# The SBUF buffers of a two-block transformer kernel in a new order

## The chip, the cores and the metric

The kernel runs on one core of a Trainium2 chip. The metric is the device time of one execution in microseconds.

## The reference

Input x has 256 tokens of 1,024 features. The first block has two layers. Each is an FFN, a mixer of four attention kinds, and another FFN:

```
x = x + 0.5 * swiglu(rms_norm(x, g1), w_gate, w_up, w_down)      # D_FF = 2816
pa, pb, pc, pd = split(rms_norm(x, gm) @ w_in)                   # 2464 columns
x = x + concat([neighbourhood(pa), mla(pb), diff(pc), gqa(pd)]) @ w_out
x = x + 0.5 * swiglu(rms_norm(x, g2), w_gate2, w_up2, w_down2)
x = rms_norm(x, gf)
```

The second block is one layer on the same tokens:

```
u = rms_norm(x, g) @ w_in_2                                      # 7424 columns
ya, yb, yc = pool(u) * silu(.), sliding_window(u) * silu(.), block_attention(u) * silu(.)
merged = ga * (ya @ w_proj_a) + gb * (yb @ w_proj_b) + gc * (yc @ w_proj_c)
out = rms_norm(x + merged @ w_out_2, gf_2)
```

All of it is float32.

## The kernel before

x stays in SBUF transposed (xT, 8 chunks of 128 features by 256 tokens). Nearly all of the work is products of activations with weights that are read once. A product of float32 numbers is made of three products of the faster type float32r: each factor is split into a high part (its rounded value) and a low part (the rest), and `product` adds high x high, high x low and low x high in PSUM. In the profile these are lines 442, 445 and 446, and 486, 489 and 494 where a stage begins with the high parts alone.

Weights come in slots of 128 partitions x 2,048 columns (1 MB), three slots deep. For slot r, SyncE loads raw[r % 3] (line 360) once the slot three before it has been split, ScalarE writes the high part w_hi[r % 3] (line 888) once the slot has landed and TensorE has begun an earlier slot, and VectorE writes the low part w_lo[r % 3] (line 1213). There are 81 slots for each of the two layers, and 45 for the last block. A full slot of 256-wide products is 48 matmuls.

Who streams and who is stationary depends on the stage. In the FFNs (gate, up, down), in the output product of the mixers and in the last block's z, gate and branch products, the weights are stationary (128 columns at a time) and hT (normed activations, transposed) or act (the gated product) streams, 256 columns. In the token projections ("proj", "tproj", function `token_proj`) hT is stationary and the weights stream, 256 columns. In the last block's output product the weights stream, 512 columns at a time. In the profile a group is named out<-streamed,stationary.

The order of the steps of a mixer is written out by hand (ORDER, ORDER2), and every engine runs through it in its own queue, with semaphores between them. The FFNs are loops.

Buffers in SBUF are made by `sb(...)` in the order of the program text, each at the next multiple of 32 bytes behind the one before. The first one, xT, begins at byte 4,224 of each partition: 4,096 bytes for descriptors (`dynamic_dma_scratch_size=4096` in the call) and four small constants lie ahead of it. PSUM tensors and all views of the buffers are unchanged by the diff.

Of the kernel before, what the change touches and what calls it, by code (L numbers as in the profile page):

```python
# [7 lines left out]
F32R = mybir.dt.float32r  # L8
# [5 lines left out]
P = 128  # L14
S = 256
T = S // P
# [17 lines left out]
PW = W1  # L34
# [4 lines left out]
RING = 3  # L39
SLOT = 2048  # L40
# [8 lines left out]
I_ID, I_MC, I_MS, I_GC, I_GS, I_NA, I_MB, I_MM, NCONST = 0, 128, 192, 256, 384, 512, 576, 832, 1088  # L49
# [84 lines left out]
def build(nc, a):  # L134
    with ExitStack() as ctx:
        def sb(name, shape, dt=F32):
            return ctx.enter_context(nc.sbuf_tensor(name, shape, dt))
# [2 lines left out]
            return ctx.enter_context(nc.semaphore(name))  # L140


        xT = sb("xT", [P, DC, S])
        hn = sb("hn", [P, T, D])
        hT_hi = sb("hT_hi", [P, DC, S], F32R)
        hT_lo = sb("hT_lo", [P, DC, S], F32R)
        act_hi = sb("act_hi", [P, 2, 2, S], F32R)
        act_lo = sb("act_lo", [P, 2, 2, S], F32R)
        proj = sb("proj", [P, T, PW])
        up_buf = sb("up_buf", [P, 2048])  # L150
        qkT = [sb(f"qkT{i}", [P, 8, S]) for i in range(2)]
        probs = [sb(f"probs{i}", [P, 4, S]) for i in range(2)]
# [1 line left out]
        bias_buf = sb("bias_buf", [P, 3072])  # L154
        scratch = sb("scratch", [P, 1536])
        pooledT = sb("pooledT", [P, 4, S])
        row = sb("row", [P, NROW])
        cols_buf = sb("cols", [P, L + 1, NCOL])
        gain2 = sb("gain2", [P, L, DC])
        const = sb("const", [P, NCONST])  # L160
        stat = sb("stat", [P, 96])
        half = sb("half", [P, 32])
        ones = sb("ones", [P, P])
        smx = sb("smx", [P, 2, 4])
        ssum = sb("ssum", [P, 2, 4])
        sinkx = sb("sinkx", [P, 2, 4])
        lam = sb("lam", [P, 4])
        xr = sb("xr", [P, 4])
        diag = sb("diag", [P, 4, P])
        mla_rope = sb("mla_rope", [P, 2, T * 2 * 32])  # L170
        r_row = sb("r_row", [P, 2, S])
        raw = [sb(f"raw{i}", [P, SLOT]) for i in range(RING)]
        w_hi = [sb(f"w_hi{i}", [P, SLOT], F32R) for i in range(RING)]
        w_lo = [sb(f"w_lo{i}", [P, SLOT], F32R) for i in range(RING)]

        t5 = qkT[0][0:32, 0:3, :].rearrange("p c s -> p (c s)")

# [1686 lines left out]
```

How the kernel before makes its waits and increments, by code:

```python
        def wait_tr_full(eng, f):  # L306
            eng.wait_ge(tr_full[f % 2], f // 2 + 1)
# [1 line left out]
        def wait_tr_done(eng, first, n):  # L309
            for f in range(max(first, first + n - 2), first + n):
                eng.wait_ge(tr_free[f % 2], f // 2 + 1)
# [1 line left out]
        def wait_pj_full(eng, f):  # L314
            eng.wait_ge(pj_full[f % 2], f // 2 + 1)
# [1 line left out]
        def wait_pj_free(eng, f):  # L317
            eng.wait_ge(pj_free[f % 2], f // 2 + 1)
# [24 lines left out]
        @block.sync  # L343
# [14 lines left out]
            def load(slot_view, src, r, l, i=None):  # L358
                sp.wait_ge(lo_set, number_of(r, l, i))
                sp.dma_start(slot_view, src).then_inc(raw_in[r % RING], 16)
# [11 lines left out]
                with sp.Fori(0, FB // 2) as i:  # L372
                    for k in range(2):
                        pos = base + 2 + 3 * k
                        load(colslot(pos), cols(wg, l, i * 512 + (k + 1) * 256), pos, l, i)
                        load(colslot(pos + 1), cols(wu, l, i * 512 + (k + 1) * 256), pos + 1, l, i)
                        load(rowslot(pos + 2), rows(wd, l, i * 512 + k * 256), pos + 2, l, i)
                load(rowslot(base + 32), rows(wd, l, (FB - 1) * 256), base + 32, l)
            for l in range(L):
                ffn(l, FFN1_AT, a["ffn1_w_gate"], a["ffn1_w_up"], a["ffn1_w_down"])
                sp.wait_ge(rpb_skew[l], 16 * 8)
                sp.dma_start(bias_buf[:, 1536:3072], a["rpb_skewed"][l]).then_inc(nab_in, 16)
                if l == 0:
                    sp.wait_ge(t5_skew, 16)
```

## Time and profile before

| | us |
|---|---|
| median of 3 runs | 1352.24 |
| lowest, highest | 1350.92, 1352.86 |
| profiled execution, its time | 1345.35 |
| its span, first to last instruction | 1343.1 |
| TensorE busy | 1293.2 |
| VectorE busy | 834.5 |
| ScalarE busy | 640.0 |
| GpSimd busy | 76.4 |

The mean granted TensorE clock of the profiled execution is 0.977. Matmuls overlap, so TensorE's busy time says only that one was under way; how fast they follow each other is read from their starts or from their count in a window.

### The profile page before, as it was taken

Reading aid. Unit: us, or ns where it says so; the run is one execution under the profiler, and the core shown is the slowest. Engines: PE = TensorE matmul, PEld = TensorE weight load, DVE = VectorE, ACT = ScalarE, POOL = GpSimd, SP = SyncE. Lnnn points to the kernel's source line nnn. Section 1 sums busy time; section 2 is a strip of 40 time slices with the busy share of each in tenths; the row PEclk is TensorE's granted clock in tenths of the full one; section 3 lists DMA queues with packets and bytes.
Section 4 is the critical chain, followed back from the end, with each engine's and each line's share of the span. In section 5 each row is a group of like instructions: output and inputs, shape, how many; then the busy total and the mean of one; then the engine's idle time right before and its main releaser. Section 6 shows DMA issues by size and latency. Waiting matters only on the chain.

```text
span 1343.1 us, 24747 instructions
## 1 busy us (share of the span) xinstructions
PE 1293.2 (96%) x10496; PEld 1266.5 (94%) x10496; DVE 834.5 (62%) x1057; ACT 640.0 (48%) x850; POOL 76.4 (6%) x57
## 2 busy tenths in 40 slices
PE   6999999988999999999999997999999989999997
PEld 6999999987999999999999996899999989899996
DVE  5755567755665555875557675586555664446665
ACT  4433346745533334533334764553333544666542
POOL 1110011200000000000001120000000000000000
PEclk9999999987999999999999997899999999999999
DMA  8776565320565555565565540256555655415542
GB/s 281 222 208 201 184 220 156 126 94 4 186 189 188 187 187 181 165 198 188 187 201 156 166 139 29 67 181 193 188 187 187 196 158 178 136 50 161 182 146 108
DMA packets 169514, 220.34 MB, mean 164 GB/s; under 512 B 5280, under 2 KB 152480, under 8 KB 169312
## 3 DMA queue, kind: packets, MB, share of 16 engines
q1 hardware_dynamic: 165680, 213.66, 50.0%
q0 software_dynamic: 2080, 2.48, 0.9%
q10 hardware_dynamic: 1680, 3.13, 0.7%
q8 instruction: 56, 0.92, 0.3%
q14 instruction: 18, 0.15, 0.0%
HBM read 218.15 MB, written 3.42 MB: 165 GB/s over the span
## 4 chain that ended last, share of the span: by engine, by line
PE 86%; ACT 6%; DVE 5%; issue 1%; DMA 1%; POOL 0%; SPq 0%; POOLq 0%; DVEq 0%; ACTq 0%
PE pj L442 12%; PE pj L446 12%; PE pj L445 12%; PE acc L442 8%; PE acc L446 8%; PE acc L445 8%; PE tr L442 6%; PE tr L446 6%; PE tr L445 6%; PE acc L625 3%; ACT probs L1016 2%; DVE w_lo L1213 1%; ACT w_hi L888 1%; PE tr L617 1%; PE acc L605 1%
## 5 line engine op out<-in xcount | busy, mean ns | idle before, releaser
L1213 DVE TENSOR_TENSOR w_lo<-raw,w_hi 128x2048 fp32r<-128x2048 f32 (+2 forms) x206 | 458.4, 2226 | 249.2 <-ACT w_hi L888 247.8
L888 ACT ACTIVATE w_hi<-raw 128x2048 fp32r<-128x2048 f32 (+2 forms) x206 | 380.8, 1852 | 419.4 <-PE pj L442 151.0
L442 PE MATMUL pj<-hT_hi,w_hi 128*128 128x256 f32 x992 | 279.7, 282 | 1.3 <-DVE w_lo L1213 1.1
L446 PE MATMUL pj<-hT_hi,w_lo 128*128 128x256 f32 x992 | 278.2, 280 | 0.0
L445 PE MATMUL pj<-hT_lo,w_hi 128*128 128x256 f32 x992 | 278.1, 280 | 0.0
L446 PE MATMUL acc<-act_hi,w_lo 128*128 128x256 f32 x704 | 197.3, 280 | 0.0
L442 PE MATMUL acc<-act_hi,w_hi 128*128 128x256 f32 x704 | 197.3, 280 | 0.0
L445 PE MATMUL acc<-act_lo,w_hi 128*128 128x256 f32 x704 | 197.3, 280 | 0.0
L442 PEld LDWEIGHTS pj<-hT_hi,w_hi 128*128 128x128 f32 x992 | 186.9, 188 | 2.8 <-DVE w_lo L1213 1.3
L445 PEld LDWEIGHTS pj<-hT_lo,w_hi 128*128 128x128 f32 x992 | 186.9, 188 | 0.0
L446 PEld LDWEIGHTS pj<-hT_hi,w_lo 128*128 128x128 f32 x992 | 186.8, 188 | 0.0
L442 PE MATMUL tr<-hT_hi,w_hi 128*128 128x256 f32 x640 | 181.1, 283 | 2.4 <-DVE scratch L1317 2.4
L445 PE MATMUL tr<-hT_lo,w_hi 128*128 128x256 f32 x640 | 180.1, 281 | 0.0
L446 PE MATMUL tr<-hT_hi,w_lo 128*128 128x256 f32 x640 | 180.1, 281 | 0.0
L442 PEld LDWEIGHTS acc<-act_hi,w_hi 128*128 128x128 f32 x704 | 132.6, 188 | 0.0
L445 PEld LDWEIGHTS acc<-act_lo,w_hi 128*128 128x128 f32 x704 | 132.6, 188 | 0.0
L446 PEld LDWEIGHTS acc<-act_hi,w_lo 128*128 128x128 f32 x704 | 132.6, 188 | 0.0
L442 PE MATMUL pj<-w_hi,hT_hi 128*128 128x256 f32 (+1 forms) x448 | 127.9, 285 | 0.5 <-ACT proj L1039 0.5
L446 PE MATMUL pj<-w_hi,hT_lo 128*128 128x256 f32 (+1 forms) x448 | 126.3, 282 | 0.0
L445 PE MATMUL pj<-w_lo,hT_hi 128*128 128x256 f32 (+1 forms) x448 | 125.9, 281 | 0.0
L442 PEld LDWEIGHTS tr<-hT_hi,w_hi 128*128 128x128 f32 x640 | 121.3, 190 | 3.7 <-DVE scratch L1317 3.3
L445 PEld LDWEIGHTS tr<-hT_lo,w_hi 128*128 128x128 f32 x640 | 121.2, 189 | 0.3 <-issue 0.2
(214 smaller groups left out, 1970.6 us busy)
## 6 DMA issues: line engine op xcount, KB each, us to landing
raw<-in_w_in SPq DMA_DIRECT2D x47, 1024.0 KB, 5.4
raw<-in_ffn_w_up SPq DMA_DIRECT2D x44, 1024.0 KB, 5.4
raw<-in_ffn_w_down SPq DMA_DIRECT2D x44, 1024.0 KB, 5.0
raw<-in_ffn_w_gate SPq DMA_DIRECT2D x43, 1024.0 KB, 5.4
raw<-in_w_out SPq DMA_DIRECT2D x12, 1024.0 KB, 4.9
raw<-in_w_proj_a SPq DMA_DIRECT2D x4, 512.0 KB, 3.5
raw<-in_w_proj_b SPq DMA_DIRECT2D x4, 512.0 KB, 3.5
raw<-in_w_proj_c SPq DMA_DIRECT2D x4, 512.0 KB, 3.4
```

The source lines that it names most:

```text
L442: ins = pe.matmul(out, lhs[0], rhs[0], start=first, stop=False, **kw)
L445: pe.matmul(out, lhs[0], rhs[1], start=False, stop=False, **kw)
L446: return pe.matmul(out, lhs[1], rhs[0], start=False, stop=last, **kw)
L605: ins = pe.matmul(ps[:, h, 0:nk * P], q, k, start=True, stop=True)
L617: ins = pe.transpose(bank[:, j, :], probs[u % 2][:, h, kt * P:(kt + 1) * P], ident)
L625: ins = pe.matmul(ps[:, 0, h * 64:(h + 1) * 64], probsT[u % 2][:, h, kt, :], v(h, kt), start=(kt == 0), stop=(kt == nk - 1))
L888: act.activation(w_hi[r % RING][:, 0:w], raw[r % RING][:, 0:w], ACT.Copy).then_inc(hi_set, 1)
L1016: ins = act.activation(probs[u % 2][:, h, 0:nk * P], src[:, h, 0:nk * P], ACT.Exp, bias=smx[:, u % 2, h:h + 1], scale=scale, accum_out=ssu ...
L1213: dve.tensor_tensor(w_lo[r % RING][:, 0:w], raw[r % RING][:, 0:w], w_hi[r % RING][:, 0:w].bitcast(F32), ALU.subtract).then_inc(lo_set, 1)
```

## The change

The buffers are made in another order: first the large ones whose size is a multiple of 2,048 bytes, with the nine weight buffers (raw, w_hi, w_lo) right behind act_lo, then proj, then the small ones. Sizes, views, instructions, waits and transfers stay the same. The last byte used is the same within 32.

```
-        proj = sb("proj", [P, T, PW])
+        raw = [sb(f"raw{i}", [P, SLOT]) for i in range(RING)]
+        w_hi = [sb(f"w_hi{i}", [P, SLOT], F32R) for i in range(RING)]
+        w_lo = [sb(f"w_lo{i}", [P, SLOT], F32R) for i in range(RING)]
         up_buf = sb("up_buf", [P, 2048])
         qkT = [sb(f"qkT{i}", [P, 8, S]) for i in range(2)]
         probs = [sb(f"probs{i}", [P, 4, S]) for i in range(2)]
...
         bias_buf = sb("bias_buf", [P, 3072])
         scratch = sb("scratch", [P, 1536])
         pooledT = sb("pooledT", [P, 4, S])
+        diag = sb("diag", [P, 4, P])
+        r_row = sb("r_row", [P, 2, S])
+        proj = sb("proj", [P, T, PW])
+        const = sb("const", [P, NCONST])
+        ones = sb("ones", [P, P])
+        stat = sb("stat", [P, 96])
+        half = sb("half", [P, 32])
+        mla_rope = sb("mla_rope", [P, 2, T * 2 * 32])
         row = sb("row", [P, NROW])
         cols_buf = sb("cols", [P, L + 1, NCOL])
         gain2 = sb("gain2", [P, L, DC])
-        const = sb("const", [P, NCONST])
-        stat = sb("stat", [P, 96])
-        half = sb("half", [P, 32])
-        ones = sb("ones", [P, P])
         smx = sb("smx", [P, 2, 4])
         ssum = sb("ssum", [P, 2, 4])
         sinkx = sb("sinkx", [P, 2, 4])
         lam = sb("lam", [P, 4])
         xr = sb("xr", [P, 4])
-        diag = sb("diag", [P, 4, P])
-        mla_rope = sb("mla_rope", [P, 2, T * 2 * 32])
-        r_row = sb("r_row", [P, 2, S])
-        raw = [sb(f"raw{i}", [P, SLOT]) for i in range(RING)]
-        w_hi = [sb(f"w_hi{i}", [P, SLOT], F32R) for i in range(RING)]
-        w_lo = [sb(f"w_lo{i}", [P, SLOT], F32R) for i in range(RING)]
```

The starts in bytes, worked out from the sizes (float32 and float32r have 4 bytes) and the rule of 32 above:

| buffer | size | before | mod 2048 | mod 64 | after | mod 2048 | mod 64 |
|---|---|---|---|---|---|---|---|
| xT | 8192 | 4224 | 128 | 0 | 4224 | 128 | 0 |
| hn | 8192 | 12416 | 128 | 0 | 12416 | 128 | 0 |
| hT_hi | 8192 | 20608 | 128 | 0 | 20608 | 128 | 0 |
| hT_lo | 8192 | 28800 | 128 | 0 | 28800 | 128 | 0 |
| act_hi | 4096 | 36992 | 128 | 0 | 36992 | 128 | 0 |
| act_lo | 4096 | 41088 | 128 | 0 | 41088 | 128 | 0 |
| raw0 to raw2 | 3 x 8192 | 142304 | 992 | 32 | 45184 | 128 | 0 |
| w_hi0 to w_hi2 | 3 x 8192 | 166880 | 992 | 32 | 69760 | 128 | 0 |
| w_lo0 to w_lo2 | 3 x 8192 | 191456 | 992 | 32 | 94336 | 128 | 0 |
| up_buf to pooledT | 63488 | 64896 | 1408 | 0 | 118912 | 128 | 0 |
| diag | 2048 | 137184 | 2016 | 32 | 182400 | 128 | 0 |
| r_row | 2048 | 140256 | 992 | 32 | 184448 | 128 | 0 |
| proj | 19712 | 45184 | 128 | 0 | 186496 | 128 | 0 |
| const | 4352 | 131648 | 576 | 0 | 206208 | 1408 | 0 |
| ones | 512 | 136512 | 1344 | 0 | 210560 | 1664 | 0 |
| stat | 384 | 136000 | 832 | 0 | 211072 | 128 | 0 |
| half | 128 | 136384 | 1216 | 0 | 211456 | 512 | 0 |
| mla_rope | 1024 | 139232 | 2016 | 32 | 211584 | 640 | 0 |
| row | 2568 | 128384 | 1408 | 0 | 212608 | 1664 | 0 |
| cols | 588 | 130976 | 1952 | 32 | 215200 | 160 | 32 |
| gain2 | 64 | 131584 | 512 | 0 | 215808 | 768 | 0 |
| smx, ssum, sinkx, lam, xr | 128 | 137024 | 1856 | 0 | 215872 | 832 | 0 |

In the last line the start is that of smx; ssum and lam begin 32 bytes past a multiple of 64 in both orders. The group from up_buf to pooledT keeps its inner order.

## Rows read from the trace of the kernel before

**Rows 1.** Part 1 of the page: busy us, share of the span, instructions.
```profile
PE 1293.2 (96%) x10496; PEld 1266.5 (94%) x10496; DVE 834.5 (62%) x1057; ACT 640.0 (48%) x850; POOL 76.4 (6%) x57
```

**Rows 2.** The chain that ended last, shares of the span by engine.
```profile
PE 86%; ACT 6%; DVE 5%; issue 1%; DMA 1%; POOL 0%; SPq 0%; POOLq 0%; DVEq 0%; ACTq 0%
```

**Rows 3.** Line 442: durations (ns min/median/max), first and last start, forms; who waited.
```profile
L442 PE MATMUL pj<-hT_hi,w_hi x992: 277/281/468, 17.6 to 1303.0; 128*128 128x256 f32 x199
...
L442 PE MATMUL pj<-w_hi,hT_hi x448: 235/281/682, 209.8 to 1190.5; 128*128 128x256 f32 x140, 128*128 128x160 f32 x10
...
  ACT w_hi L888: 405.5, 125
```

**Rows 4.** Windows: length, busy us and count by engine, granted clock, DMA share, GB/s.
```profile
366.00:548.00 182.00, 182.00 (x1536) 181.99 (x1534) 113.97 (x102) 77.08 (x62) 0.00 (x0) 1.00 0.57 184
892.00:1074.00 182.00, 182.00 (x1535) 182.00 (x1534) 113.75 (x102) 76.94 (x62) 0.00 (x0) 1.00 0.59 190
557.00:728.00 171.00, 171.00 (x1458) 170.92 (x1457) 111.99 (x114) 69.09 (x49) 3.51 (x1) 1.00 0.60 191
...
1126.50:1310.00 183.50, 179.66 (x1511) 175.82 (x1510) 103.64 (x172) 105.09 (x168) 0.00 (x0) 1.00 0.45 140
```

**Rows 5.** Timeline, TensorE: start us, duration us, instruction; ends of two runs.
```profile
1114.95 0.28 PE L442 MATMUL pj<-w_hi,hT_hi 128*128 128x256 f32 x1
...
1126.47 0.28 PE L442 MATMUL pj<-hT_hi,w_hi 128*128 128x256 f32 x1
...
1323.07 0.40 PE L442 MATMUL acc<-w_hi,hT_hi 128*128 128x512 f32 x1
...
1334.04 0.40 PE L446 MATMUL acc<-w_hi,hT_lo 128*128 128x512 f32 x1
```

**Rows 6.** TensorE's groups by form: count, busy us, mean ns, idle before, releaser.
```profile
L442 PE MATMUL pj<-hT_hi,w_hi 128*128 128x256 f32 x992 | 279.7, 282 | 1.3 <-DVE w_lo L1213 1.1 <-DVE scratch L1608 0.2
L442 PE MATMUL acc<-act_hi,w_hi 128*128 128x256 f32 x704 | 197.3, 280 | 0.0
L442 PE MATMUL tr<-hT_hi,w_hi 128*128 128x256 f32 x640 | 181.1, 283 | 2.4 <-DVE scratch L1317 2.4
L442 PE MATMUL pj<-w_hi,hT_hi 128*128 128x256 f32 x416 | 119.1, 286 | 0.5 <-ACT proj L1039 0.5
...
L442 PE MATMUL acc<-w_hi,hT_hi 128*128 128x512 f32 x32 | 12.8, 399 | 0.0
```

**Rows 7.** VectorE's and ScalarE's groups by form, same columns.
```profile
L1303 DVE TENSOR_TENSOR act_lo<-proj,act_hi 128x512 fp32r<-128x512 f32 x44 | 30.5, 692 | 1.5
L1299 DVE TENSOR_TENSOR proj<-proj,r_row 128x512 f32<-128x512 f32 x44 | 30.5, 692 | 1.5
...
L888 ACT ACTIVATE w_hi<-raw 128x2048 fp32r<-128x2048 f32 x190 | 363.1, 1915 | 414.0 <-PE pj L442 145.5 <-PE acc L442 135.2 <-PE tr L442 119.3
...
L900 ACT ACTIVATE hn<-xT 128x2048 f32<-128x2048 f32 x7 | 13.3, 1903 | 0.0
```

**Rows 8.** DMA issues: count, KB each, median us from issue to landing.
```profile
raw<-in_ffn_w_up SPq DMA_DIRECT2D x44, 1024.0 KB, 5.4
raw<-in_ffn_w_down SPq DMA_DIRECT2D x44, 1024.0 KB, 5.0
...
t_skewed<-t_line POOLq DMA_DIRECT2D x1, 768.0 KB, 10.8
```

**Rows 9.** Waits of ScalarE: us in total, times, longest us.
```profile
ACT w_hi L888 <- DMA raw<-in_ffn_w_gate: 6.1, 2, 5.0
```

**Rows 10.** The chain that ended last, near the start: start us, us, what.
```profile
5.10 8.18 DMA raw<-in_ffn_w_up
```

**Rows 11.** The same chain in layer 0's mixer.
```profile
254.00 0.87 PE tr L617 x8
```

## The prediction

> **What bounds the kernel now.** The page's busy table comes first: TensorE is busy for 1293.2 of 1343.1 us, VectorE for 62% and ScalarE for 48% [rows 1]. The chain that ended last agrees: 86% of it is TensorE, 6% ScalarE, 5% VectorE, 1% DMA [rows 2]. So the time is mostly the number of matmuls times the distance from one start to the next. A matmul's recorded duration doesn't give that distance: it is 281 ns at the median whether hT or the weights stream through the array [rows 3], and the next matmul has long begun when it ends. The spacing has to be counted, in stretches where TensorE never stops.
>
> - First FFN of layer 1 (hT or act streams, weights are stationary), 557 to 728 us: 1,458 matmuls touch the window, about two of them begun before it, so 171.0 / 1,456 = 117.4 ns [rows 4].
> - Second FFN, 366 to 548 us in layer 0 and 892 to 1074 in layer 1, the same code on the same buffers: 182.0 / 1,534 = 118.6 ns [rows 4].
> - Token projections of the last block (weights stream, hT is stationary): tproj 4 and tproj 2 have 96 matmuls between the starts at 1114.95 and 1126.47 us, 120.0 ns [rows 5].
> - Last product, 512 columns wide, weights stream: 47 matmuls between 1323.07 and 1334.04 us, 233.4 ns [rows 5].
>
> The granted clock is 1.00 in these windows, the 2.4 GHz level, at which 256 columns are 106.7 ns and 512 are 213.3. So a 256-column product takes 10.7 to 13.3 ns more than its columns, and the 512-column one 20.1 ns more. That excess is what a change of addresses could touch. It is large: the three big groups with hT or act streaming hold (992 + 704 + 640) x 3 = 7,008 matmuls, and the one with weights streaming 416 x 3 = 1,248 [rows 6]. One nanosecond on these 8,256 is 8.3 us, 0.6%. I leave the smaller groups out of the sums.
>
> **The change, part by part.** No instruction, wait or transfer is added, removed or reordered, so all counts stay. Only the starts move. By the table of starts, raw, w_hi and w_lo go from 32 past a multiple of 64 bytes (992 modulo 2048) to a multiple of 64 (128 modulo 2048); diag, r_row and mla_rope also lose their 32; hT and act stay put; cols, ssum and lam stay 32 past. Four kinds of user follow.
>
> *VectorE and ScalarE.* The trace holds both placements already. A 512-column product with r_row, 32 bytes off, takes 692 ns, and the one with only aligned buffers (act_lo) 692. ScalarE's 2048-column pass over a slot, 32 off, takes 1915 ns, the aligned one over xT 1903 [rows 7]. So the price is 0 to 12 ns an instruction. Even 12 ns on all 190 copies of slots is 2.3 us of ScalarE time, under 414.0 us of idle time ahead of them [rows 7], most of it spent waiting for TensorE (405.5 us in 125 waits [rows 3]). I take 0; without that cover it would be a gain of up to 2.3 us.
>
> *Transfers.* A 1 MB slot lands 5.0 to 5.4 us after its issue [rows 8], one is needed every 48 x 117.4 ns = 5.6 us, and it is asked for ahead of need: the largest group of ScalarE's waits for a slot's landing is 6.1 us in two waits [rows 9]. Exposed is only the start, where the chain holds 8.18 us of the second slot's load [rows 10]. At the 5.0 us of the same size elsewhere it would save 3.2 us; at 10.8, the longest landing of any transfer [rows 8], it would lose 2.6. Those are the ends; I take 0, since that load is slow for company (eight loads of xT and of the first slot are issued just before it), not for its target. The Trainium skill ("DMA: Bandwidth & Descriptors", How a descriptor splits into AXI transactions) says a descriptor that starts off a multiple of 256 bytes costs extra beats: my estimate from that page is 39 beats for 1,024 bytes at the old offset and 36 at the new one. No row here shows beats; by it the exposed load would gain under a microsecond.
>
> *GpSimd and small tables.* GpSimd works on stat, half and xr, a few columns each, and is 1% or less of the chain [rows 2]; 0.
>
> *TensorE's reads.* Here the trace speaks on both sides. For an effect: weights streaming, 32 off, against an aligned hT go at 120.0 ns, while an aligned hT streaming against off-placed weights goes at 117.4 or 118.6, with the same shape, type and pattern of three products [rows 4, 5]. Only addresses and roles differ. Against an effect: first and second FFN read the very same addresses and still differ by 1.2 ns, so something besides placement (how loads and matmuls fall into step after a stop) picks the level too. And within 557 to 728 us halves and chunks of a slot set the two operands at distances that differ by multiples of 512 bytes, while VectorE is busy for 112 us and ScalarE for 69, and the level holds.
>
> The Trainium skill ("SBUF — State Buffer", Who interferes with whom) gives TensorE two independent read ports and says it never waits on anyone; by it no layout has a price and the sum is zero. The windows agree as far as other engines' work goes; they don't decide between TensorE's own two reads.
>
> I take the favourable step: once all operands of these products start on a multiple of 64, long runs go at 117.4 ns, the lowest spacing that a 256-column product holds over a stretch here.
> - Token projections: 1,248 x 2.6 ns = 3.2 us.
> - The two second FFNs: 2 x 1,534 x 1.2 ns = 3.7 us.
> - Last block: 15 z and gate slots of 48 and 12 branch slots of 24 follow the start at 1126.47 us, 1,008 matmuls among the 1,511 of that window [rows 4]; I assume 118.6 for them, x 1.2 = 1.2 us.
> - The 512-column product: 32 x 3 x an assumed 2 ns = 0.2 us.
>
> The sum is 8.3 us. The profiled execution took 1345.35 us with a span of 1343.1, and would take 1337. The median of the runs shown is 1352.24, 6.9 above it, so the forecast is 1352.2 - 8.3 = **1344 us**, with 1340 to 1349 as that case's own range (upper end: the token projections alone gain).
>
> **Rivals.**
>
> *Nothing happens.* How a run falls into step sets the level, and it falls as before. For it: the two FFN levels repeat in both layers at equal addresses, and VectorE and ScalarE don't care about 32 bytes. Against it: the token projections stand apart at 120.0. Time 1352. One stretch that falls otherwise by chance moves it by 1,534 x 1.2 = 1.8 us.
>
> *Slower: the two operands now start in the same place.* hT and a weight chunk will begin at equal offsets modulo 512; so far they differ by 352. If TensorE's two reads get in each other's way when they start together, the good level is lost. All at 120.0 costs (7,008 - 3,068 - 1,008) x 2.6 = 7.6 and 4,076 x 1.4 = 5.7, together 13.3 us: 1366. It decides against the change as soon as the two first FFNs fall by one step (2 x 1,456 x 1.2 = 3.5 us, 1356), more than the token projections could give back. For it: equal code can run at 118.6. Against it: shifts of 512 bytes between the operands do nothing today.
>
> *Much faster: the whole excess is the 32 bytes.* The nearest row of a low spacing is 8 transposes of 128 columns, all operands aligned, in 0.87 us, 109 ns each [rows 11]. All 8,256 products going from some 118.3 to 109 would give 77 us: 1275; half of it 1314. For it: an excess that grows with width (10.7 or more at 256, 20.1 at 512) needs a cause. Against it: where hT or act streams, the streamed operand is aligned already and the excess is there; and an excess per column is no sign of a start address. The Trainium skill ("TensorE: Matmul & The Clock Gate", Back-to-back issue gap) gives the columns plus 2.5 ns for an isolated matmul, 109.2 ns here; no FFN product of the trace keeps to it.
>
> **How the numbers follow.** What a measurement of this kernel can tell from no change is 0.2%, 2.7 us. The forecast has a chance of 0.36, much faster 0.08, nothing 0.34, slower 0.22. A little of the forecast's case ends within the bound (one gain alone), and a little of "nothing" outside it, so: faster 0.43, same 0.35, slower 0.22. The range reaches over no change into both outer cases, past the two first FFNs' loss on one side and the half-way value of "much faster" nearly on the other: 1322 to 1359. About 0.15 is left out.
>
> **What would show it.** After the change: the 96 matmuls of tproj 4 and 2 in 11.27 us in place of 11.52; about 1,550 matmuls in 182 us of the second FFN in place of 1,536; the last product's spacing below 233 ns. VectorE's and ScalarE's times for a slot and the 5.0 to 5.4 us to landing stay. The prediction is wrong if the three spacings stay where they are (nothing) or the first FFN leaves 117.4 upward (slower). Its mechanism is wrong, whatever the time, if a gain comes from the start or from ScalarE's waits for transfers.

## The result: slower by 0.7%

| kernel | median us | lowest, highest | executions |
|---|---|---|---|
| before | 1351.93 | 1344.61, 1358.19 | 12 |
| after | 1361.90 | 1355.08, 1367.87 | 12 |

The ratio is 1.0073, with a 95% interval of 1.004 to 1.0106. The profiled execution of the changed kernel took 1367.55 us with a span of 1365.2 and a mean granted clock of 0.968. The forecast was 1344 and the range 1322 to 1359: the rival "slower" came true.

All line numbers of the product are one higher than before (L443, L446, L447). The page's busy table and the shares of the chain that ended last:

```profile
PE 1317.2 (96%) x10496; PEld 1291.1 (95%) x10496; DVE 834.5 (61%) x1057; ACT 639.8 (47%) x850; POOL 76.4 (6%) x57
...
PE 86%; ACT 6%; DVE 5%; issue 1%; DMA 1%; POOL 0%; SPq 0%; POOLq 0%; DVEq 0%; ACTq 0%
```

The counts are those of [rows 1] and the shares those of [rows 2]. Only TensorE grew, by 24.0 us of busy time. The groups by form of VectorE and ScalarE, which answer to [rows 7]:

```profile
L1304 DVE TENSOR_TENSOR act_lo<-proj,act_hi 128x512 fp32r<-128x512 f32 x44 | 30.5, 693 | 1.5
L1300 DVE TENSOR_TENSOR proj<-proj,r_row 128x512 f32<-128x512 f32 x44 | 30.5, 692 | 1.5
...
L889 ACT ACTIVATE w_hi<-raw 128x2048 fp32r<-128x2048 f32 x190 | 362.7, 1912 | 428.8 <-PE pj L443 153.8 <-PE acc L443 143.9 <-PE tr L443 122.5
...
L901 ACT ACTIVATE hn<-xT 128x2048 f32<-128x2048 f32 x7 | 13.3, 1900 | 0.0
```

A pass over a slot that no longer sits 32 bytes off takes 1912 ns where it took 1915, and the product with r_row stays at 692: these two engines show no effect of the move. The transfers of a slot, beside [rows 8]:

```profile
raw<-in_ffn_w_up SPq DMA_DIRECT2D x44, 1024.0 KB, 5.4
raw<-in_ffn_w_down SPq DMA_DIRECT2D x44, 1024.0 KB, 5.0
```

Nor do they. The exposed load of the second slot is 8.12 us in the chain against 8.18 [rows 10]. That leaves the spacing of the matmuls. The four windows of [rows 4], same columns:

```profile
366.00:548.00 182.00, 182.00 (x1518) 181.94 (x1518) 110.56 (x94) 68.62 (x46) 2.67 (x1) 1.00 0.57 185
892.00:1074.00 182.00, 182.00 (x1517) 181.94 (x1517) 112.66 (x100) 72.87 (x54) 2.67 (x1) 1.00 0.57 184
557.00:728.00 171.00, 169.73 (x1410) 169.07 (x1409) 109.05 (x100) 65.88 (x45) 6.51 (x2) 1.00 0.58 189
1126.50:1310.00 183.50, 179.99 (x1490) 175.79 (x1490) 98.31 (x163) 104.41 (x169) 0.00 (x0) 1.00 0.44 139
```

The granted clock is 1.00 as before, and the second FFNs get 1,518 and 1,517 matmuls into 182 us in place of 1,536 and 1,535: 182.0 / 1,516 = 120.0 ns. The third window is off by the later start of its stage and has a stop in it; a window that lies wholly in the first FFN of layer 1 is shown with the experiments, and gives 120.0 too. The two runs in which weights stream, beside [rows 5]:

```profile
1136.84 0.28 PE L443 MATMUL pj<-w_hi,hT_hi 128*128 128x256 f32 x1
...
1148.36 0.28 PE L443 MATMUL pj<-hT_hi,w_hi 128*128 128x256 f32 x1
...
1340.15 0.39 PE L443 MATMUL acc<-w_hi,hT_hi 128*128 128x512 f32 x1
...
1345.59 0.39 PE L443 MATMUL acc<-w_hi,hT_hi 128*128 128x512 f32 x1
```

Token projections: 96 matmuls in 11.52 us, 120.0 ns, exactly as before. The 512-column product: 24 matmuls in 5.44 us, 226.7 ns where it had 233.4. So 120.0 ns is now the spacing of every 256-column product, and only the 512-column one gained.

**Where the time went, slot by slot.** I matched the 207 slots of the two traces and took the time from each slot's first matmul to the next slot's. The whole slots without a stop (7,320 matmuls of 256 columns) took 13.2 us more, the last product 0.6 us less, all the rest 9.8 us more. That makes the 22 us between the two spans. The 9.8 us are in the mixers and at stops, about half of them in one long slot of layer 0's mixer (54.6 us before, 59.2 after). A window there, of before and then of after:

```profile
300.00:360.00 60.00, 53.91 (x403) 50.59 (x403) 37.95 (x76) 33.87 (x74) 3.03 (x3) 0.85 0.22 71
```
```profile
300.00:360.00 60.00, 53.54 (x324) 49.66 (x323) 26.99 (x61) 26.91 (x67) 3.03 (x3) 0.72 0.17 52
```

The granted clock is 0.85 of the 2.4 GHz level in one and 0.72 in the other, because more of the 60 us was spent at the 1.2 GHz level; the engine has gaps before and within that stretch in both. This part differs between executions of one kernel. The new places of the mixers' own buffers are another candidate, but e3 and e6 below share that order, and outside the whole slots their traces took 1.4 us less and 2.1 us more than before's. The changed kernel ran 1355.1 us with a mean clock of 0.977 and 1367.9 with 0.970. Before's profiled execution has 0.977 as well, and took 1345.35: 9.8 us less at an equal clock. The measured 10 us, with an interval of 5.4 to 14.3, are compatible with the 12.6 that the slots show, so no second cause is called for.

### The profile page after: what moved, and what is told of

The parts are those of the page before. It is cut to its first block, busy times and chain, and to the rows that moved or that the text cites. A ratio compares the mean times of both kernels' runs of the same rounds, so it can differ in the third digit from the quotient of the medians.

```text
span 1365.2 us, 24747 instructions
## 1 busy us (share of the span) xinstructions
PE 1317.2 (96%) x10496; PEld 1291.1 (95%) x10496; DVE 834.5 (61%) x1057; ACT 639.8 (47%) x850; POOL 76.4 (6%) x57
## 4 chain that ended last, share of the span: by engine, by line
PE 86%; ACT 6%; DVE 5%; issue 1%; DMA 1%; POOL 0%; SPq 0%; POOLq 0%; DVEq 0%; ACTq 0%
PE pj L443 12%; PE pj L446 12%; PE pj L447 12%; PE acc L443 8%; PE acc L447 8%; PE acc L446 8%; PE tr L443 6%; PE tr L447 6%; PE tr L446 6%; PE acc L626 4%; ACT probs L1017 2%; DVE w_lo L1214 1%; ACT w_hi L889 1%; PE tr L618 1%; PE tr L596 1%
## 5 line engine op out<-in xcount | busy, mean ns | idle before, releaser
L443 PE MATMUL pj<-hT_hi,w_hi 128*128 128x256 f32 x992 | 282.2, 284 | 1.6 <-DVE w_lo L1214 1.4
L446 PE MATMUL pj<-hT_lo,w_hi 128*128 128x256 f32 x992 | 280.7, 283 | 0.0
L447 PE MATMUL pj<-hT_hi,w_lo 128*128 128x256 f32 x992 | 280.7, 283 | 0.0
L447 PE MATMUL acc<-act_hi,w_lo 128*128 128x256 f32 x704 | 199.2, 283 | 0.0
L446 PE MATMUL acc<-act_lo,w_hi 128*128 128x256 f32 x704 | 199.2, 283 | 0.0
L443 PE MATMUL acc<-act_hi,w_hi 128*128 128x256 f32 x704 | 199.2, 283 | 0.0
L443 PEld LDWEIGHTS pj<-hT_hi,w_hi 128*128 128x128 f32 x992 | 190.3, 192 | 3.0 <-DVE w_lo L1214 1.6
L446 PEld LDWEIGHTS pj<-hT_lo,w_hi 128*128 128x128 f32 x992 | 190.4, 192 | 0.0
L447 PEld LDWEIGHTS pj<-hT_hi,w_lo 128*128 128x128 f32 x992 | 190.3, 192 | 0.0
L443 PE MATMUL tr<-hT_hi,w_hi 128*128 128x256 f32 x640 | 183.4, 287 | 2.4 <-DVE scratch L1318 2.4
L447 PE MATMUL tr<-hT_hi,w_lo 128*128 128x256 f32 x640 | 182.2, 285 | 0.0
L446 PE MATMUL tr<-hT_lo,w_hi 128*128 128x256 f32 x640 | 182.2, 285 | 0.0
L443 PEld LDWEIGHTS acc<-act_hi,w_hi 128*128 128x128 f32 x704 | 135.2, 192 | 0.0
L446 PEld LDWEIGHTS acc<-act_lo,w_hi 128*128 128x128 f32 x704 | 135.2, 192 | 0.0
L447 PEld LDWEIGHTS acc<-act_hi,w_lo 128*128 128x128 f32 x704 | 135.2, 192 | 0.0
L443 PE MATMUL pj<-w_hi,hT_hi 128*128 128x256 f32 (+1 forms) x448 | 129.0, 288 | 0.0
L443 PEld LDWEIGHTS tr<-hT_hi,w_hi 128*128 128x128 f32 x640 | 124.0, 194 | 3.7 <-DVE scratch L1318 3.3
L446 PE MATMUL pj<-w_lo,hT_hi 128*128 128x256 f32 (+1 forms) x448 | 127.2, 284 | 0.0
L447 PE MATMUL pj<-w_hi,hT_lo 128*128 128x256 f32 (+1 forms) x448 | 127.1, 284 | 0.0
L446 PEld LDWEIGHTS tr<-hT_lo,w_hi 128*128 128x128 f32 x640 | 123.9, 194 | 0.4 <-issue 0.2
```

The costliest lines, as they stand in the source:

```text
L443: ins = pe.matmul(out, lhs[0], rhs[0], start=first, stop=False, **kw)
L446: pe.matmul(out, lhs[0], rhs[1], start=False, stop=False, **kw)
L447: return pe.matmul(out, lhs[1], rhs[0], start=False, stop=last, **kw)
```

## The experiments

The theories at the start:

- **Distance.** What counts is where the weights start relative to the activations (hT or act), modulo some power of two. By the table of starts the distance is 352 modulo 512 before and 0 after.
- **Own start.** What counts is where each buffer starts by itself, or whether it is aligned.
- **Place.** What counts is where the rings lie in SBUF, or the offset of raw as a target of transfers.

All spacings below come from the traces as above: the mean over whole slots without a stop. "d" is the start of w_hi and w_lo minus that of hT and act, in bytes, modulo 256 (why 256 is shown below). The four FFN values are layer 0 first and second, layer 1 first and second. Where the three products of a group have different distances, d lists all three.

| kernel | d | FFN spacings, ns | token proj. of the last block | 512 columns | us (executions) |
|---|---|---|---|---|---|
| before | 96 | 117.3, 118.7, 117.3, 118.7 | 120.0 | 233.3 | 1351.93 (12) |
| after | 0 | 120.0 in all | 120.0 | 226.7 | 1361.90 (12) |
| e5_all_32_on | 0 | 120.0 in all | 120.0 | 226.7 | 1361.76 (1) |
| e1_rings_32_on | 32 | 118.3 in all | 116.7 | 233.3 | 1347.10 (11) |
| e4_acts_32_on | 32 | 118.3 in all | 116.6 | 233.3 | 1347.14 (1) |
| e9_rings_48_on | 48 | 117.8 in all | 118.3 | 233.3 | 1352.37 (1) |
| e6_rings_64_on | 64 | 117.8, 113.3, 113.3, 113.3 | 117.8 | 233.4 | 1324.25 (6) |
| e3_raw_32_on | 64 | 117.8, 113.3, 113.3, 113.3 | 117.8 | 228.9 | 1318.78 (1) |
| e8_rings_320_on | 64 (320) | 117.8, 113.3, 117.8, 113.3 | 117.8 | 228.9 | 1329.04 (1) |
| e12_before_gap_224 | 64 | 117.8 in all | 117.8 | 228.9 | 1339.47 (9) |
| e10_rings_80_on | 80 | 118.8, 118.7, 118.8, 118.8 | 118.4 | 231.1 | 1351.85 (1) |
| e7_rings_96_on | 96 | 117.3, 118.7, 118.7, 117.3 | 120.0 | 233.3 | 1348.41 (1) |
| e2_before_aligned | 128 | 118.7 in all | 118.7 | 232.2 | 1351.29 (12) |
| e11_rings_192_on | 192 | 117.8 in all | 117.8 | 233.3 | 1333.50 (1) |
| e13_low_parts_64_on | 0, 192, 64 | 117.8 in all | 117.8 | 231.1 | 1349.62 (1) |
| e14_w_hi_64_on | 64, 64, 0 | 117.8 in all | 118.9 | 233.3 | 1345.34 (1) |

A single execution can be some 7 us off its kernel's median either way, as the lists of before and after show (9 us in e12); with one, the spacings carry the verdict and not the time. The ratios below are against executions of before made beside each group, with medians of 1354.17 us (22 executions, e1 to e4), 1353.16 (10, e5 to e8), 1351.78 (14, e9 to e12) and 1351.95 (1, e13 and e14). Each kernel has one trace, so how its levels vary from execution to execution was not seen.

### First four: distance, own start or place

**e1_rings_32_on**, the changed kernel with 32 bytes ahead of the rings, so that the weights start at 160 modulo 2048 and hT and act stay at 128:

```
         act_lo = sb("act_lo", [P, 2, 2, S], F32R)
+        sb("gap", [P, 8])
         raw = [sb(f"raw{i}", [P, SLOT]) for i in range(RING)]
...
         w_lo = [sb(f"w_lo{i}", [P, SLOT], F32R) for i in range(RING)]
+        sb("gap2", [P, 8])
```

> The changed layout with the nine weight buffers moved on by 32 bytes (they start 32 past a multiple of 64, as before the change), everything else on multiples of 64 as in the changed kernel. Theory A, the start within 64 bytes: the first FFN goes back from 120.0 to 117.4 ns a product, the second to 118.6, the 512-column product back from 226.7 to 233.4, and the time to some 1352 us. Theory B, the place of the rings right behind the activations (or the lost distance of 97 KB): the spacing stays at 120.0 and the time at some 1362. Theory C, equal offsets of streamed and stationary operand modulo 2048 or 512: also back to 117.4, since 32 bytes part them; the next kernel tells it from A.

**e2_before_aligned**, the order of before with 32 bytes ahead of raw, so that every operand starts at a multiple of 64, but d is 128:

```
         r_row = sb("r_row", [P, 2, S])
+        sb("gap", [P, 8])
         raw = [sb(f"raw{i}", [P, SLOT]) for i in range(RING)]
```

> The layout of the kernel before with one gap of 32 bytes ahead of raw, so that the weight buffers start on a multiple of 64, still last in SBUF, 1024 modulo 2048, that is 384 modulo 512 away from hT and act. Theory A (start within 64 bytes): all FFN products at 120.0 ns, the 512-column one at 226.7, time some 1360 us. Theory B (place) and theory C (equal offsets modulo 512 or 2048): spacings of the kernel before, 117.4 and 118.6, time 1352.

**e3_raw_32_on**, the changed kernel with raw at 160 and w_hi, w_lo at 192 modulo 2048 (one gap of 32 bytes ahead of raw and one ahead of w_hi):

```
+        sb("gap", [P, 8])
         raw = [sb(f"raw{i}", [P, SLOT]) for i in range(RING)]
+        sb("gap2", [P, 8])
         w_hi = [sb(f"w_hi{i}", [P, SLOT], F32R) for i in range(RING)]
```

> The changed layout with raw alone 32 past a multiple of 64; w_hi, w_lo and all behind them on multiples of 64. If TensorE's reads are the cause, nothing changes against the changed kernel: 120.0 ns and a span of some 1350 to 1365 us. If the target of the weight transfers, or what ScalarE and VectorE read, is the cause, the first FFN is at 117.4.

**e4_acts_32_on**, the changed kernel with the activations at 160 and the weights at 192, so with both moved and d at 32:

```
         hn = sb("hn", [P, T, D])
+        sb("gap", [P, 8])
         hT_hi = sb("hT_hi", [P, DC, S], F32R)
...
         act_lo = sb("act_lo", [P, 2, 2, S], F32R)
+        sb("gap2", [P, 8])
         raw = [sb(f"raw{i}", [P, SLOT]) for i in range(RING)]
```

> The changed layout with hT_hi, hT_lo, act_hi and act_lo 32 past a multiple of 64 and the weight buffers on multiples of 64. If what helps is a stationary operand that starts 32 off while the streamed one is aligned, the roles swap: the token projections (hT stationary) fall from 120.0 to some 117.4 to 118.6 ns, the FFNs (hT and act streaming, 32 off) stay at 120.0. If only the difference of the two starts modulo 64 matters, both the FFNs and the token projections are at 117.4 to 118.6. The 512-column product (aligned weights stream) stays at 226.7 or falls.

Measured, e1: 0.9947 of before, 0.9929 to 0.9966. e2: 0.9991, 0.997 to 1.0013, no difference that can be told. e3 and e4 have one execution each, 1318.78 and 1347.14 us. Windows that lie inside the FFNs in every kernel (400 to 530 us is the second FFN of layer 0, 600 to 700 the first of layer 1), first of e1, then of e4, then of e2:

```profile
400.00:530.00 130.00, 130.00 (x1101) 130.00 (x1100) 76.37 (x63) 48.27 (x31) 0.00 (x0) 1.00 0.56 185
600.00:700.00 100.00, 100.00 (x847) 100.00 (x847) 57.98 (x48) 37.55 (x24) 0.00 (x0) 1.00 0.58 186
```
```profile
400.00:530.00 130.00, 130.00 (x1101) 130.00 (x1100) 76.39 (x64) 48.31 (x31) 0.00 (x0) 1.00 0.57 186
600.00:700.00 100.00, 100.00 (x847) 100.00 (x847) 58.27 (x46) 36.05 (x24) 0.00 (x0) 1.00 0.57 185
```
```profile
400.00:530.00 130.00, 130.00 (x1098) 130.00 (x1097) 76.03 (x64) 48.26 (x31) 0.00 (x0) 1.00 0.56 186
600.00:700.00 100.00, 100.00 (x845) 100.00 (x845) 58.38 (x46) 36.12 (x24) 0.00 (x0) 1.00 0.56 185
```

A window's count includes some two matmuls that began before it, so 1,101 is 130.0 / 1,099 = 118.3 ns. The point is that e1 and e4 have the same counts, to the matmul, though every operand of e4 starts 32 bytes further on: they share only d = 32. And e2 falsifies the step of my forecast by itself: all operands start at multiples of 64, and no stretch is at 117.4. It is at 118.7, neither the 120.0 of after, whose operands are aligned in the same way. So own start, in steps of 32 bytes, is out. The distance doesn't count modulo 128, since 128 and 0 differ (of the two, e2 alone has the old order). The time of e1 is less clear than its spacings: the traces of e1 and before differ by 1.4 us, at clocks of 0.973 and 0.977, and the whole slots by 0.2 us, since the token projections gained and the first FFNs lost. Where the 0.5% of the medians comes from isn't shown. e3 was meant to test raw's offset as a transfer's target; it moved d to 64 by the way, and its one execution was over 20 us below every one of e1, e2 and e4. That asked for its own test. In e1 the token projections, with the roles swapped, have 96 matmuls between these starts, 11.20 us or 116.7 ns:

```profile
1114.49 0.28 PE L445 MATMUL pj<-w_hi,hT_hi 128*128 128x256 f32 x1
...
1125.69 0.28 PE L445 MATMUL pj<-hT_hi,w_hi 128*128 128x256 f32 x1
```

### The next four: which distance, and modulo what

**e5_all_32_on**, the changed kernel with everything from hT_hi on 32 bytes further (d stays 0), **e6_rings_64_on**, with the rings alone 64 further, **e7_rings_96_on** (96) and **e8_rings_320_on** (320). Each has one gap:

```
         hn = sb("hn", [P, T, D])
+        sb("gap", [P, 8])        # e5 alone
         hT_hi = sb("hT_hi", [P, DC, S], F32R)
...
         act_lo = sb("act_lo", [P, 2, 2, S], F32R)
+        sb("gap", [P, 16])       # e6 ([P, 24] in e7, [P, 80] in e8; none in e5)
         raw = [sb(f"raw{i}", [P, SLOT]) for i in range(RING)]
```

> The changed layout with hT_hi and everything behind it 32 bytes on: the distance stays 0 modulo 2048, and both operands start 32 past a multiple of 64. Theory C: as the changed kernel, 120.0 ns for 256 columns in all roles and 226.7 for the 512-column product, span 1345 to 1365 us. Theory A (each operand's own start within 64 bytes): another spacing, 117 to 119 ns.

> The changed layout with the weight buffers and all behind them 64 bytes on: all on multiples of 64, w_hi and w_lo 64 bytes from hT and act modulo 2048, raw too. In the last call the same distance, with raw at 32 past a multiple of 64, gave 113.3 and 117.8 ns and a span of 1316.5 us. Theory C (what counts is the distance between the streamed and the stationary operand): 113.3 ns for most FFN slots, 1316 to 1330 us. Theory D (raw off by 32 gave it, through the transfers or through ScalarE and VectorE): 120.0 ns, some 1362 us.

> The changed layout with the rings 96 bytes on: distance 96, the same as in the kernel before modulo 128 and modulo 256 (there it is 864 modulo 1024, 352 modulo 512). If the distance counts modulo 256 or less, the spacings of the kernel before come back exactly: 117.3 for first FFNs, 118.7 for second ones, 120.0 for token projections, 233.3 for the 512-column product, span some 1343 us. If it counts modulo 512, they differ.

> The changed layout with the rings 320 bytes on: distance 320, which is 64 modulo 256 and modulo 128, but not modulo 512. If the distance counts modulo 256 or less: 113.3 ns for most FFN slots, as at distance 64. If it counts modulo 512: another value, 116 to 120.

Measured: e6 took 1324.25 us (1320.14 to 1332.28), 0.9808 of before with an interval of 0.9764 to 0.9851. The same windows and, where they add something, 100 to 190 us (first FFN of layer 0) and 900 to 1030 us (second FFN of layer 1). After itself:

```profile
400.00:530.00 130.00, 130.00 (x1086) 130.00 (x1085) 76.66 (x62) 46.08 (x30) 0.00 (x0) 1.00 0.55 180
600.00:700.00 100.00, 100.00 (x836) 100.00 (x835) 59.99 (x52) 35.65 (x23) 0.00 (x0) 1.00 0.55 179
```

e5:

```profile
400.00:530.00 130.00, 130.00 (x1086) 130.00 (x1085) 75.88 (x61) 47.32 (x30) 0.00 (x0) 1.00 0.57 185
600.00:700.00 100.00, 100.00 (x835) 100.00 (x835) 59.36 (x53) 37.46 (x24) 0.00 (x0) 1.00 0.58 186
```

e6:

```profile
100.00:190.00 90.00, 90.00 (x766) 90.00 (x766) 53.93 (x43) 33.78 (x22) 6.83 (x5) 1.00 0.64 205
400.00:530.00 130.00, 130.00 (x1149) 130.00 (x1149) 79.97 (x65) 50.16 (x32) 0.00 (x0) 1.00 0.60 192
600.00:700.00 100.00, 100.00 (x884) 100.00 (x884) 61.95 (x49) 37.69 (x24) 3.52 (x1) 1.00 0.62 201
900.00:1030.00 130.00, 130.00 (x1149) 130.00 (x1148) 79.45 (x64) 49.97 (x32) 0.00 (x0) 1.00 0.60 194
```

e7:

```profile
400.00:530.00 130.00, 130.00 (x1098) 130.00 (x1097) 75.41 (x60) 47.06 (x31) 0.00 (x0) 1.00 0.57 183
600.00:700.00 100.00, 100.00 (x845) 100.00 (x844) 58.26 (x48) 37.62 (x24) 0.00 (x0) 1.00 0.57 185
900.00:1030.00 130.00, 130.00 (x1111) 130.00 (x1110) 81.91 (x68) 49.98 (x32) 0.00 (x0) 1.00 0.57 186
```

e8:

```profile
400.00:530.00 130.00, 130.00 (x1149) 130.00 (x1149) 79.29 (x67) 51.33 (x35) 0.00 (x0) 1.00 0.59 193
600.00:700.00 100.00, 100.00 (x851) 100.00 (x850) 59.87 (x48) 36.66 (x24) 0.00 (x0) 1.00 0.60 195
900.00:1030.00 130.00, 130.00 (x1150) 130.00 (x1149) 80.89 (x65) 50.24 (x32) 0.00 (x0) 1.00 0.61 198
```

- e5 against after: equal counts but for one matmul, again with everything moved by 32. Distance 0 costs 120.0 ns at both starts.
- e6 against after: 64 bytes between the same buffers, and 1,149 matmuls fit where 1,086 did, 130.0 / 1,147 = 113.3 ns. Slot by slot e6 gains 24.4 us on before in whole slots (7,368 matmuls). It is also e3 without e3's raw, with the same FFN and token levels: the target of the transfers plays no part in them. The 512-column product differs between the two, 233.4 and 228.9 ns, which isn't explained.
- e8 at 320 has the levels of 64. e7 at 96 has all of before's (117.3, 118.7, 120.0, 233.3), and before is at 352. So, as sets of levels, the distance counts modulo 256.
- e7 shows something else: its first FFN of layer 1 is at 118.7 and its second at 117.3, the reverse of before. At one distance a whole stretch sits at either of two levels. At d = 64 they are 117.8 and 113.3 (e6's first window is at 90.0 / 764 = 117.8, and e8's middle one at 117.8 where e6 had 113.3).

### Four more: the old order, the other side, and sixteen bytes

**e12_before_gap_224** is the order of before with 224 bytes ahead of raw, which makes d 64:

```
         r_row = sb("r_row", [P, 2, S])
+        sb("gap", [P, 56])
         raw = [sb(f"raw{i}", [P, SLOT]) for i in range(RING)]
```

> The kernel before with one gap of 224 bytes ahead of raw and no other change: the rings stay last in SBUF, and the distance between them and hT or act becomes 1088, 64 modulo 256. Theory C (the distance modulo 256): 113.3 and 117.8 ns in the FFNs, 1320 to 1330 us, 0.98 of before. Theory B (the new order itself): as before, 117.3 to 118.7 ns and 1352 us.

**e11_rings_192_on** is the changed kernel with d = 192, which is 64 on the other side:

```
+        sb("gap", [P, 48])
         raw = [sb(f"raw{i}", [P, SLOT]) for i in range(RING)]
```

> The changed layout with the rings 192 bytes on, distance 192, that is -64 modulo 256. If the sign of the distance matters (streamed minus stationary), the roles at distance 64 swap. At distance 64 both roles showed 113.3 and 117.8 ns, so this should show the same two levels: FFNs at 113.3 or 117.8, token projections at 117.8 or 113.4, a span of 1316 to 1335 us. If only a positive distance of the weights helps: 117 to 120 ns.

**e9_rings_48_on** and **e10_rings_80_on** make each ring one buffer, with its slots 16 bytes in, so that d can be 48 and 80 (16 in place of 8 in e10's gap):

```
+        sb("gap", [P, 8])
+        def ring(name, dt=F32):
+            all_ = sb(name, [P, RING * SLOT + 4], dt)
+            sb(name + "_gap", [P, 56])
+            return [all_[:, 4 + i * SLOT:4 + (i + 1) * SLOT] for i in range(RING)]
...
+        raw, w_hi, w_lo = ring("raw"), ring("w_hi", F32R), ring("w_lo", F32R)
```

> The changed layout with w_hi, w_lo and raw at distance 48 (each ring one tensor with its slots 16 bytes in, and 256 bytes more from ring to ring). Between 32 (118.3 ns) and 64 (113.3 or 117.8). If the distance counts in whole steps of 32 or 64 bytes, it equals 118.3; if it counts byte for byte, it lies between, 115 to 118.

> As the kernel at distance 48, at distance 80: between 64 (113.3 or 117.8 ns) and 96 (117.3 or 118.7). If whole steps of 32 or 64 bytes count, it equals distance 64; if byte for byte, it lies between.

Measured: e12 took 1339.47 us (1333.36 to 1348.59), 0.9898 of before with an interval of 0.9864 to 0.9933. The same two windows of e12, and one in the output product of layer 1's mixer:

```profile
400.00:530.00 130.00, 130.00 (x1106) 130.00 (x1106) 77.54 (x63) 48.27 (x31) 0.00 (x0) 1.00 0.57 186
600.00:700.00 100.00, 100.00 (x851) 100.00 (x851) 58.18 (x46) 36.76 (x24) 0.00 (x0) 1.00 0.58 183
...
861.00:878.00 17.00, 17.00 (x152) 17.00 (x152) 13.50 (x20) 12.32 (x13) 0.00 (x0) 1.00 0.49 165
```

The old order gains too once d is 64, by about 1%. In this trace all four FFNs sit at the upper level of d = 64, 117.8, while the output products of both mixers (the third window, 17.0 / 150 = 113.3) and several stretches of the last block are at 113.4. So the 1% isn't won in the FFNs, whose 117.8 is next to the mean of before's 117.3 and 118.7: whole slots give 5.5 us of the 11.8 between the two spans, and the rest lies in slots with a stop and isn't accounted for.

e11 has the same 117.8 in the FFNs. Of its token projections in the mixers some are at 113.5 and others at 117.8; in e12 one is at 113.3 and the others are at 117.8. e9 and e10 give nothing: 117.8 and 118.8 in the FFNs. e9 also has runs at 123.3, the slowest 256-column level of all kernels, in the output product of layer 1's mixer and in the last block, where the other kernels are at 113.4 to 120.0. One such window, 34.0 / 276 = 123.2 ns:

```profile
1284.00:1318.00 34.00, 34.00 (x278) 34.00 (x277) 21.40 (x21) 15.99 (x14) 0.00 (x0) 1.00 0.49 162
```

So moving the weights on by 16 bytes counts as well, and 64 is not the middle of a broad valley. But in e9 and e10 alone the weights start 16 bytes off a multiple of 32, so a price of that start is not told from one of the distance. And the level at one distance isn't a matter of the distance alone.

### The last two: which pair of the three products

The products hi x hi, lo x hi and hi x lo follow each other with loads of weights in between. At distance 0 two things could meet: the stream of one product and the load of the next one's weights, or something between a product's stream and its own weights. The next two kernels give the three pairs different distances.

**e13_low_parts_64_on**, the changed kernel with hT_lo, act_lo and w_lo 64 bytes on. A product's own pairs then have distances 0, 192 and 64, while each stream and the following weights are at 0 throughout:

```
         hT_hi = sb("hT_hi", [P, DC, S], F32R)
+        sb("g1", [P, 16])
         hT_lo = sb("hT_lo", [P, DC, S], F32R)
+        sb("g2", [P, 48])
         act_hi = sb("act_hi", [P, 2, 2, S], F32R)
+        sb("g3", [P, 16])
         act_lo = sb("act_lo", [P, 2, 2, S], F32R)
+        sb("g4", [P, 48])
         raw = [sb(f"raw{i}", [P, SLOT]) for i in range(RING)]
         w_hi = [sb(f"w_hi{i}", [P, SLOT], F32R) for i in range(RING)]
+        sb("g5", [P, 16])
```

> The changed layout with hT_lo, act_lo and w_lo 64 bytes on; hT_hi, act_hi and w_hi at distance 0 modulo 256, and so are the low parts among themselves. The three products of a term are (stationary w_hi, streamed h_hi), (w_hi, h_lo), (w_lo, h_hi). Theory C1, the streamed operand meets the load of the next matmul's weights: the pairs are h_hi with w_hi, h_lo with w_lo, h_hi with w_hi, all at distance 0, so 120.0 ns as in the changed kernel. Theory C2, it meets the load of its own weights: h_lo with w_hi and h_hi with w_lo are 64 apart, so two of three matmuls gain, some 114 to 118.5 ns.

**e14_w_hi_64_on**, w_hi alone 64 bytes on: own distances 64, 64 and 0.

```
         raw = [sb(f"raw{i}", [P, SLOT]) for i in range(RING)]
+        sb("g1", [P, 16])
         w_hi = [sb(f"w_hi{i}", [P, SLOT], F32R) for i in range(RING)]
+        sb("g2", [P, 48])
```

> The changed layout with w_hi alone 64 bytes on, w_lo at distance 0. By either theory two pairs of three are at distance 64 and one at 0: the spacing lies between that of distance 64 (113.3 or 117.8 ns) and 120.0. If it is at 120.0, the worst pair alone sets it; if at 113.3 to 117.8, w_hi alone does.

Measured, one execution each: e13 1349.62 us, e14 1345.34. The two windows of e13, then of e14:

```profile
400.00:530.00 130.00, 130.00 (x1106) 130.00 (x1105) 75.59 (x60) 48.25 (x31) 0.00 (x0) 1.00 0.57 186
600.00:700.00 100.00, 100.00 (x852) 100.00 (x851) 58.83 (x48) 36.44 (x23) 0.00 (x0) 1.00 0.57 184
```
```profile
400.00:530.00 130.00, 130.00 (x1107) 130.00 (x1105) 77.48 (x63) 48.22 (x31) 0.00 (x0) 1.00 0.57 186
600.00:700.00 100.00, 100.00 (x851) 100.00 (x851) 58.19 (x46) 36.72 (x24) 0.00 (x0) 1.00 0.57 183
```

Both are at 117.8 ns in all four FFNs. e13 rules out the stream against the next load as I stated it: that pair is at distance 0 in all three products, and the spacing isn't 120.0. The own pair is consistent with both kernels. But e13 also moves the low parts against the high ones, and e14 w_hi against w_lo, and every load overlaps the stream before it in the trace, so I call the own pair favoured and not shown. In neither trace did any long run reach 113.3. That all three pairs have to be 64 apart for it isn't shown either, since e12 has all three so and its FFNs are at 117.8.

## Why the prediction was wrong, point by point

- **TensorE's spacing is all there is to win or lose**: right. The counts, VectorE's and ScalarE's durations, the landings and the start stayed as forecast, at 0.
- **"I take the favourable step: once all operands of these products start on a multiple of 64, long runs go at 117.4"**: the step that failed. It took the start of each operand for the cause. e5 (same distance, all starts moved: same 120.0), e4 beside e1 (same distance, same counts) and e2 (aligned, 118.7) show that it is the distance between the two, modulo 256 by e7 and e8. Its four terms were to give 8.3 us; the token projections gave 0 (120.0 before and after), and the second FFNs and the last block lost 1.3 ns a matmul in place of gaining 1.2. The largest loss had no term at all: the step held the first FFNs at 117.4 because they had the lowest spacing, and they went to 120.0, 2 x 1,462 x 2.7 ns = 7.9 us.
- **The 512-column product below 233 ns**: right in sign, by luck, and larger than the assumed 2 ns, for which no row stood: 6.6 ns, 0.6 us in all. Alignment isn't the reason: e5, all 32 off, has 226.7 too, and e2, all aligned, 232.2. Distance 0 is the best seen for 512 columns and the worst of the 256-column FFN levels.
- **The rival "slower: the two operands now start in the same place"**: its condition and its sum held; that two reads get in each other's way fits, and isn't shown. It gave all at 120.0 and 13.3 us; the slots show 120.0 and 13.2. Its 1366 us is 4 above the median of 1361.90. Of that the last product's gain is 0.6 and the base 0.3 (1352.24 for 1351.93); the rest is within the interval of 5.4 to 14.3 us.
- **The argument against that rival**, "shifts of 512 bytes between the operands do nothing today", was sound as a row and wrong as a reason: 512 is a multiple of 256, so it left the distance as it was. The trace of before held no pair at another distance with the roles kept, and the chance of 0.22 was too small for a mechanism that named the one number of the change (352 to 0) that no row had tried.
- **"Something besides placement picks the level too"**: right. e7 and before have equal distances and levels, in another order of stretches.
- **"Much faster"** (77 us, half of it 38) did not come, and not by alignment. Another layout, e6, gained 1.9%, some 26 us, by distance; its best level is 113.3 ns. 109 ns was held over a long run by none of the kernels.
- **"0.2%, 2.7 us"** as what can be told from no change was too fine: twelve executions of each kernel gave an interval of 0.33% to each side.

The Trainium skill ("SBUF — State Buffer", Who interferes with whom) gives TensorE two independent read ports and lets it wait on nobody. By it every row of the table would have one spacing. The runs differ, 113.3 to 120.0 ns in the FFNs, in kernels that differ by gaps and the order of buffers alone, and the measurement decides.

One row bears on where a level changes. In e12 the output product of layer 1's mixer goes at 117.8 ns from 848.2 us on; four transposes come in between at 859.24, and behind them the same product goes at 113.4 for 166 matmuls, with the same distance:

```profile
859.12 0.28 PE L447 MATMUL acc<-hT_hi,w_lo 128*128 128x256 f32 x1
859.24 0.60 PE L596 MATMUL tr<-const,hn 128*128 128x128 f32 x4
859.60 0.37 PE L443 MATMUL acc<-hT_hi,w_hi 128*128 128x256 f32 x1
```

So the level can change where other matmuls break into a run. Over the 1,400 and more matmuls of an FFN that follow each other unbroken, it didn't.

What stays open: what picks one of the two levels for a stretch, and what in TensorE's reads meets at distance 0. In six executions of e6 the span was 1317.8 to 1322.2 four times and 1328.6 and 1330.0 twice, at clocks between 0.967 and 0.970. One FFN stretch at 117.8 in place of 113.3 is 1,534 x 4.5 ns = 6.9 us, which would fit; only one execution was traced, so it isn't shown.

The best of the kernels with several executions is e6, the changed layout with 64 bytes between act_lo and raw: 0.981 of before (0.9764 to 0.9851), so better than both. e3 has the same FFN levels and had one execution, 1318.78.

## What to carry to other kernels

Where a stage is bound by back-to-back float32r matmuls, treat the distance between the streamed and the stationary buffer as a parameter, and try a few gaps of 32 to 192 bytes ahead of one of them, and judge by the level as well as by the distance, since one distance gave two: here the same instructions took 1324 or 1362 us. Large buffers of round sizes laid out side by side all start in the same place modulo 256, which gave the two slowest times of this kernel's layouts (after 1361.90, e5 1361.76). Count matmuls in a window with no stop, since durations of single ones and busy shares don't show such an effect, and when a row shows that a shift does nothing, ask which shifts its argument has really tried.

## What the runs showed of the hardware

- In the FFNs a 128 x 256 float32r product follows the one before every 120.0 ns at d = 0, 118.3 at 32, 117.8 or 113.3 at 64, 117.3 or 118.7 at 96 and 118.7 at 128, with the granted clock at 1.00 throughout. The 128 x 512 product has 226.7 at d = 0 and 228.9 to 233.4 elsewhere.
- It is not symmetric in roles: at d = 32 the token projections, weights streaming, have 116.7 against 118.3.
- A level holds for a whole FFN of some 1,500 matmuls once it has begun: the means of its slots stay within 0.3 ns (0.5 in e13).
- VectorE, ScalarE and the transfers show no effect of 32 bytes (692 and 692 ns, 1915 and 1912, 5.0 to 5.4 us to landing in both).
